# A decoder block with 32 experts: attention's order of work, the hgrn share in three products, and the first expert's rows per tile

## Time and profile before

| | us |
|---|---|
| median of 3 runs | 1307.71 (1305.7 to 1308.83) |
| the profiled execution's own time | 1308.46 |
| its span, first to last instruction | 1306.6 |
| PE busy in the span | 1248.9 (96%) |
| DVE, ACT, POOL busy | 538.1, 238.5, 135.8 |
| mean granted TensorE clock | 0.988 of 2.4 GHz |
| DMA, mean over the span | 345 GB/s |

### The profile page before, as it was taken

How to read it: one execution, slowest core, us unless ns; L and a number is a source line. 1 busy time by engine, 2 the same in 40 slices (tenths; PEclk the granted TensorE clock), 3 DMA queues, 4 the chain that set the end, 5 groups by cost and what they waited for, 6 DMA issues and landing times.

```text
span 1306.6 us, 33478 instructions
## 1 busy us (share of the span) xinstructions
PE 1248.9 (96%) x14751; PEld 726.3 (56%) x14752; DVE 538.1 (41%) x1045; ACT 238.5 (18%) x485; POOL 135.8 (10%) x144
## 2 busy tenths in 40 slices
PE   6999999999999999999999999999999999999994
PEld 5888876675357565555444455444445454545442
DVE  5767646566424524223242333333333333242424
ACT  6364424421011111010010100010000000010102
POOL 0000001100022221221010101001010101010002
PEclk9999999998999999999999999999999999999997
DMA  9523219027899999999999999999999999999993
GB/s 294 163 65 91 72 45 408 2 114 300 348 395 417 423 415 423 411 415 424 424 424 423 424 424 422 426 422 422 423 424 423 423 424 424 424 423 425 424 390 141
DMA packets 69402, 450.87 MB, mean 345 GB/s; under 512 B 6921, under 2 KB 36077, under 8 KB 44576
## 3 DMA queue, kind: packets, MB, share of 16 engines
q1 hardware_dynamic: 64832, 438.59, 81.5%
q0 software_dynamic: 4416, 10.02, 2.4%
HBM read 441.46 MB, written 9.31 MB: 345 GB/s over the span
## 4 chain that ended last, share of the span: by engine, by line
PE 62%; DMA 32%; DVE 2%; issue 1%; ACT 1%; SPq 0%; DVEq 0%
DMA w_raw_pair<-w_down 29%; PE psum L1945 24%; PE psum L1963 14%; PE psum L1698 8%; PE psum L1695 3%; DMA w_raw_pair<-w_up 3%; PE psum L1974 2%; PE psum L1784 2%; PE psum L1832 1%; PE psum L1808 1%; PE psum L1936 1%; PE psum L1771 1%; PE psum L1849 1%; DMA x_rows<-x 1%; PE psum L2018 1%
## 5 line engine op out<-in xcount | busy, mean ns | idle before, releaser
L1945 PE MATMUL psum<-w_raw_pair,x_slots_turned 128*32 128x512 f32 x4928 | 550.4, 593 | 1.0 <-DMA w_raw_pair<-w_up 0.8
L1945 PEld LDWEIGHTS psum<-w_raw_pair,x_slots_turned 128*32 128x32 f32 x4928 | 208.8, 110 | 280.4 <-issue 218.9
L1963 PE MATMUL psum<-w_raw_pair,a_slots 128*32 128x256 f32 x4992 | 288.3, 380 | 11.7 <-DMA w_raw_pair<-w_down 10.6
L1963 PEld LDWEIGHTS psum<-w_raw_pair,a_slots 128*32 128x32 f32 x4992 | 186.3, 110 | 103.5 <-DMA w_raw_pair<-w_down 15.3
L1522 DVE TENSOR_TENSOR x_rows<-x_rows,psum 128x1024 f32<-128x1024 f32 x106 | 124.6, 1218 | 269.5 <-PE psum L1974 269.5
L845 ACT ACTIVATE lin<-psum 128x768 f32<-128x768 f32 (+1 forms) x32 | 22.5, 704 | 579.3 <-PE psum L1945 579.3
L1491 DVE STREAM_TRANSPOSE a_slots<-glu 128x768 f32<-128x768 f32 (+1 forms) x31 | 26.3, 849 | 202.6 <-PE psum L1963 202.6
L1486 DVE STREAM_TRANSPOSE x_slots_turned<-gathered_quarters 128x256 f32<-128x256 f32 x74 | 43.2, 628 | 113.7 <-PE psum L1945 113.0
L640 POOL COPY gather_quarters<-row_quarters 128x2 int32 (+1 forms) x30 | 16.4, 547 | 691.6 <-DVE x_slots_turned L1486 659.4
L1974 PEld LDWEIGHTS psum<-y_part_group,token_sel 32*128 32x128 f32 x2016 | 63.5, 184 | 42.7 <-issue 42.7
L645 POOL DMA_INDIRECT gathered_quarters<-normed_rows,gather_quarters x74 | 75.0, 1014 | 39.2 <-POOL gather_quarters L640 25.8
(11 more groups left out here) (290 smaller groups left out, 1045.9 us busy)
## 6 DMA issues: line engine op xcount, KB each, us to landing
w_raw_pair<-w_up SPq DMA_DIRECT2D x128, 2048.0 KB, 37.7
w_raw_pair<-w_down SPq DMA_DIRECT2D x64, 2048.0 KB, 37.9
w_in_raw<-w_in SPq DMA_DIRECT2D x28, 512.0 KB, 3.7
w_buf<-w_out SPq DMA_DIRECT2D x4, 1024.0 KB, 8.5
expert_rows<-zero_rows SPq DMA_DIRECT2D x5, 512.0 KB, 6.9
x_rows<-x SPq DMA_DIRECT2D x4, 512.0 KB, 5.2
x_rows<-x SPq DMA_DIRECT2D x1, 2048.0 KB, 17.4
normed_rows<-h_rows SPq DMA_DIRECT2D x4, 512.0 KB, 2.6
```

What stands on the lines that cost most here:

```text
L1945: ins = pe.matmul(U[quarter(j), g, :], slots, up_columns(w, j), start=False, stop=(c == UPC - 1))
L1963: ins = pe.matmul(banks[quarter(j), g, :], slots[:, g, 2 * c + h, :], raw[q.slot(m)][:, at_w:at_w + 256], start=False, stop=(c == DNC - 1 ...
```

## The change

Three edits in one. (1) Scores go into three buffers instead of two; the scores of heads 0 and 1 are made behind av's first slice, in recurrence head 3, and so are their maxima and exponentials; later scores are made in halves of two row tiles, a head ahead; PE turns the probabilities of head h + 1 before the pv product of head h. DVE waits for x_again before its loop over the heads, where it stood before the first add. (2) `hgrn_share` is made in three float32r products instead of one float32 product: ACT makes high parts of G and of the recurrence's half of w_out (GH, WGH), POOL the low parts (GLo, WOL[:, 0]). The shares are taken in the order 0, 2, 4, 6, 1, 3 in heads 2 to 7, share 5 before oT and share 7 behind it. GH and WGH lie where two pairs of the first expert's weights go, so SP issues these two (`FIRST 2` and `FIRST 4`) only when share 7 is full, ahead of G2. (3) The slot matrices are made for tiles 0 and 1 before DVE's last x2 add, and for 2 and 3 after the last choice; the first expert's rows are gathered tile by tile between the logits; `order` moves behind the second up chunk, and on DVE `order_experts` behind the turning of the rows.

The diff, cut to its core:

```diff
@@ -210,7 +210,10 @@
         junk = over("x_sq", [P, D], g0)
         ZR = over("zero_rows", [P, D], hg0)
-        E = over("scores", [P, 2, 1280], fk0)
+        E = [over(f"scores{n}", [P, 1280], (fk0, fk0 + 5120, hg0 + 40960)[n]) for n in range(3)]
+        WGH = over("w_hgrn_high", [P, 2, HH, 512], hg0 + 16384, F32R)
...
+        def scored_in(h):
+            pair, tiles = ((h + 2) // 2, (2, 3)) if h % 2 == 0 else ((h + 3) // 2, (0, 1))
+            return ((2 * pair, 2 * pair + 1), tiles) if pair < AH // 2 else ((), ())
         def pair_scores(h):
-            return [("qk", g, i) for g in (h, h + 1) for i in range(TT)]
-        jobs += pair_scores(0)
-        SHARES = {h: h - 1 for h in range(1, AH)}
-        W_OUT_AFTER = (1, 2, 5, 6)
+            heads, tiles = scored_in(h)
+            return [("qk", a, i) for i in tiles for a in heads]
+        share_order = [n for half in range(2) for n in range(half, 2 * TT, 2)]
+        SHARES = dict(zip(range(2, AH), share_order))
+        BEFORE_OT, BEHIND_OT = share_order[AH - 2:]
+        W_HGRN_AFTER, W_OUT_AFTER = (0, 0, 1, 2), (3, 4, 5, 6)
+        jobs += pair_scores(-1) + [("pt", 0, c) for c in range(3)]
         for h in range(AH):
-            jobs += [("pt", h, c) for c in range(3)]
...
-            if h % 2 == 0 and h + 2 < AH:
-                jobs += pair_scores(h + 2)
+            jobs += pair_scores(h)
+            if h + 1 < AH:
+                jobs += [("pt", h + 1, c) for c in range(3)]
             jobs += [("pv", h)]
...
-        jobs += [("xa", n) for n in LATE_SHARES]
-        jobs += [("oT", j) for j in range(4)]
+        jobs += [("xa", BEFORE_OT)] + [("oT", j) for j in range(4)] + [("xa", BEHIND_OT)]
...
@@ -556,8 +574,10 @@
             load_pair(FIRST, 6, 6, 0)
             freed(sp, "gT", HH - 1)
             sp.dma_start(slot_rank[:, :], consts[:, CW:CW + P]).then_inc(S("slot_rank_in"), 16)
-            for n in range(0, 6, 2):
-                load_pair(FIRST, n, n, 0)
+            load_pair(FIRST, 0, 0, 0)
+            full(sp, "xa", BEHIND_OT)
+            load_pair(FIRST, 2, 2, 0)
+            load_pair(FIRST, 4, 4, 0)
...
             pool.memset(ZR[:, :], 0.0).then_inc(S("zero_rows"), 1)
+            for h in range(HH):
+                pool.wait_ge(S("g_high"), h + 1)
+                pool.tensor_tensor(GLo[:, h, :], G[:, h, :], GH[:, h, :].bitcast(F32), ALU.subtract).then_inc(S("g_low"), 1)
+            for m in range(4):
+                n, k = m // 2, m % 2 * 2
+                pool.wait_ge(S("w_hgrn_high"), m + 1)
+                pool.tensor_tensor(WOL[:, 0, n, k:k + 2, :], Wb[:, 0, n, k:k + 2, :], WGH[:, n, k:k + 2, :].bitcast(F32),
+                                   ALU.subtract).then_inc(S("w_hgrn_low"), 1)
...
                     hgrn_exps(act, h + 1)
+                if h == HH - 1:
+                    exps(0)
                 projected(h, 1)
+                if h == HH - 1:
+                    exps(1)
...
-                for c in range(3):
-                    if c == 1:
-                        continue
+            def probs_turned(h):
+                for c in (0, 2):
                     full(act, "pt", h, c)
                     if h >= 2:
                         full(act, "pv", h - 2)
                     lo, hi = (0, 512) if c == 0 else (1024, 1280)
                     act.activation(PTs[:, h % 2, lo:hi], bank("pt", h, c)[:, 0:hi - lo], ACT.Copy
                                    ).then_inc(free_sem("pt", h, c), 1)
-                if h in W_OUT_AFTER:
-                    m = W_OUT_AFTER.index(h)
+            probs_turned(0)
+            for h in range(HH):
+                freed(act, "gT", h)
+                act.activation(GH[:, h, :], G[:, h, :], ACT.Copy).then_inc(S("g_high"), 1)
+            for h in range(AH):
+                if h + 1 < AH:
+                    probs_turned(h + 1)
+                if h + 2 < AH:
+                    exps(h + 2)
+                for m in range(4):
                     n, k = m // 2, m % 2 * 2
-                    act.wait_ge(S(f"w_attn{n}"), 16)
-                    if m == 0:
-                        full(act, "o", HH - 1)
...
+            def masked_max(h, tiles):
+                for i in tiles:
+                    full(dve, "qk", h, i)
+                    n = TT * (h % 4) + i
+                    if h >= 3:
+                        full(dve, "pt", h - 3, 2)
+                    dve.tensor_tensor_reduce(E[h % 3][:, EOFF[i]:EOFF[i] + P * (i + 1)], bank("qk", h, i)[:, 0:P * (i + 1)],
+                                             cst("pairs")[:, (TT - 1 - i) * P:], 1.0, -3e38, ALU.add, ALU.max,
+                                             mx[:, n:n + 1]).then_inc(free_sem("qk", h, i), 1)
+                    freed(dve, "qk", h, i)
+                    dve.tensor_scalar(nmx[:, n:n + 1], mx[:, n:n + 1], -DH ** -0.5, None, ALU.mult
+                                      ).then_inc(S("neg_max"), 1)
             dve.wait_ge(S("c_rest"), 16)
             decays(0)
...
+                    masked_max(0, range(TT))
+                    masked_max(1, range(TT))
...
-                    masked_max(h + 2)
+            masked_max(2, (0, 1))
+            probs_turned(0)
+            masked_max(3, (0, 1))
+            dve.wait_ge(S("x_again"), 16)
+            for h in range(AH):
+                heads, tiles = scored_in(h)
                 if h in SHARES:
-                    if SHARES[h] == 0:
-                        dve.wait_ge(S("x_again"), 16)
                     add_share("xa", SHARES[h])
-                if h % 2 == 0 and h + 2 < AH:
-                    masked_max(h + 2)
+                if heads:
+                    masked_max(heads[0], tiles)
+                if h + 1 < AH:
+                    probs_turned(h + 1)
+                if heads:
+                    masked_max(heads[1], tiles)
...
                 dve.wait_ge(S("attn_high"), j + 1)
                 dve.scalar_tensor_tensor(OTL[:, j, :], bank("oT", j), agc[:, j:j + 1], OTH[:, j, :].bitcast(F32),
                                          ALU.mult, ALU.subtract).then_inc(free_sem("oT", j), 1)
+            add_share("xa", BEHIND_OT)
...
+            def slots_of(tiles):
+                cols = slice(tiles[0] * NE, (tiles[-1] + 1) * NE)
+                dve.wait_ge(S("selected"), tiles[-1] + 1)
+                link(dve.scalar_tensor_tensor(LG[:, 5, cols], bank("pos")[:, cols], 1.0, LG[:, 2, cols], ALU.add, ALU.mult))
+                for i in tiles:
+                    dve.tensor_scalar(SEL[:, i, :], slot_rank[:, :], LG[:, 5, i * NE:i * NE + 1], -1.0, ALU.subtract, ALU.is_equal
+                                      ).then_inc(sel_ready, 1)
...
+                if i == TT - 1:
+                    dve.wait_ge(S("slot_rank_in"), 16)
+                    dve.wait_ge(S("placed"), TT - 2)
+                    slots_of((0, 1))
                 add_share("x2", i, 1)
...
+            slots_of((TT - 2, TT - 1))
...
                 a_rows(p, n, As)
-            order_experts()
             slot_values()
...
                 ins = dve.transpose(xq[:, g, :, :], Xp[:, g, :].rearrange("p (i k) -> p k i", k=DK))
             ins.then_inc(t_free, 1)
+            order_experts()
+            next_rows()
             ordered()
-            next_rows()
             gates()
...
@@ -1703,6 +1768,14 @@
                 for j in range(4):
                     project(g, j)
+            def scores(heads, tiles):
+                for i in tiles:
+                    for g in heads:
...
+                    for j in range(4):
+                        freed(pe, "aq", j)
+                        freed(pe, "ak", j)
+                    scores((0, 1), range(TT))
...
             def hgrn_share(n):
-                if n == 0:
-                    for h in range(HH):
-                        freed(pe, "gT", h)
-                    pe.wait_ge(S("w_hgrn0"), 16)
-                    pe.wait_ge(S("w_hgrn1"), 16)
-                i = n // 2
+                i, half = n // 2, n % 2
+                pe.wait_ge(S("g_low"), HH)
+                pe.wait_ge(S("w_hgrn_low"), 2 * half + 2)
                 o = begin("xa", n)
-                for k in range(HH):
-                    ins = pe.matmul(o, G[:, k, i * P:(i + 1) * P], Wb[:, 0, n % 2, k, :], start=(k == 0), stop=(k == HH - 1))
+                for first, rows, w_rows in ((True, GH, WGH[:, half, :, :]), (False, GH, WOL[:, 0, half, :, :]),
+                                            (False, GLo, WGH[:, half, :, :])):
+                    for k in range(HH):
+                        ins = pe.matmul(o, rows[:, k, i * P:(i + 1) * P], w_rows[:, k, :], start=(first and k == 0),
+                                        stop=(rows is GLo and k == HH - 1))
                 ins.then_inc(full_sem("xa", n), 1)
-            attn_scores(0)
-            for h in range(AH):
+            def probs_turned(h):
                 pe.wait_ge(S("probs"), TT * (h + 1))
```

(38 more changed lines are left out.)

110 lines of the change are left out of this document (45 added, 65 removed).

## The result

The changed kernel takes 1323.5 us (median; 1321.1 to 1325.6), the kernel before 1306.7 on the same chip: the ratio is 1.0128, with a 95% interval of 1.0111 to 1.0146, so 14.5 to 19.1 us slower. A second set of runs of the same code gave 1.0131 (1.0113 to 1.0149). The forecast was 1314.7 and its range ended at 1320: the direction came, the size didn't. The profiled execution took 1322.9 and its span is 14.4 us longer than that of before.

The account below looks back on a forecast made before the run. The prediction took the chain of waits, chiefly PE's up to the first up product, as the bound, with the weight stream at its limit later. Terms +10.8 - 4.7 + 0.9 = +7.0 us gave 1314.7 us, range 1305 to 1320.

Parts of the forecast that it names:

- The first wait: Ahead of all attention heads: DVE waits for x, landing at 212.8 us, so PE stands 11.5 us, till 213.5.
- Rival (a): Transfers aren't held up by those ahead of them: x lands early, G2 takes some 5 us; 1296 us; 10%.
- Rival (d): The clock stays at 1.2 GHz behind waits through the heads' small products and first logits: 1320 us; 12%.
- The attention and G2, +10.8: Attention to first logits: oT 0.9 us later, G2 13.2 us behind two pairs; first logits 10.8 us late.
- the two long waits: PE's new waits, for x in attention and for G2 before the first x2 add: 11 and 5 us.
- The first expert's rows, -4.7: Router stage: half the last norm and row products moved earlier, so turning the rows starts sooner; 4.7 us gained.
- up to 1 us, within this term: DVE's wait for the last rows' store to normed_rows behind two pairs, ahead of turning: at most 1 us.
- order, +0.9: `order` moved behind the second up chunk now lies on PE's path: 0.9 us more.
- Rival (b): The weight stream hides the change, since DMA sets the end: 1308 us; 8%.
- What comes ahead of the first up product moves the end one for one: Until 366 us the weight stream follows PE, so changes before the first up product (318.3 us) shift the end equally.

Follow-up runs that it names:

- after: The changed kernel itself, as measured and profiled against the kernel before: 1323.5 us, ratio 1.0128.
- store_first: The changed kernel with pairs SECOND 2 and SECOND 4 issued behind the store of the last normed rows instead of ahead of it: ratio 1.0107.
- x_wait_late: The changed kernel with DVE's wait for x moved from ahead of head 0 to ahead of the first add of a share: ratio 1.0033.
- g2_first: The changed kernel with only the issue of G2 moved ahead of the pairs FIRST 2 and FIRST 4: ratio 1.0060.
- all_three: The changed kernel with the edits of store_first, x_wait_late and g2_first together: ratio 0.9926 to the kernel before.
- one_pair_one_product: one_pair_ahead with the shares as one float32 product again, without the copies and subtractions for high and low parts: ratio 0.9925.
- one_pair_ahead: all_three with SECOND 2 ahead of the last rows' store again and SECOND 4 still behind it: ratio 0.9911.
- after_again: The changed kernel run and traced once more with nothing changed: ratio 1.0131 to the kernel before.
- low_part_last: one_pair_ahead with a share's three products reordered, w_out's low part last, each waiting only for what it reads: ratio 0.9888, median 1293.6 us.
- low_last_x_early: low_part_last with x's second load issued behind the recurrence half of w_out, ahead of the attention half: ratio 0.9893.

## Why the prediction was wrong in size

What held. The first wait: x landed at 213.3 (forecast 212.8), DVE waited for it ahead of all heads, PE stood 12.3 us (11.5), and the first two low parts of w_out were ready at 221.6 (221.5). From share 0 to the end of pv 7 it was 40.1 us in the forecast and 40.1 in the trace (223.6 to 263.7): the new share is 2.8 us, and the three stalls between heads are gone. POOL's four subtractions took 4.95 us, 1.2 each, and ended at 202. G2 took 13.16 us behind its two pairs (13.2), and the first x2 add waited for it. Rival (a) fell with that, in three places: x, G2 and the store all landed as late as what was ahead of them in the queue makes them. Rival (d), the clock, was right in its mechanism and was the nearest to the time.

What failed, term by term, with the trace of after against the earlier trace rows:

- **The attention and G2, +10.8: it was +14.9** (logits of tile 0 at 296.3, 14.9 us later than before, 0.4 of it there at k_end_rows already). Share 0 came 2.0 us later than forecast (223.6 in the chain for 221.6), since behind PE's wait turns and pv 1 ran at half clock: 2.39 and 3.20 us where the later ones took 1.31 and 2.34. That gave oT 268.6 for 266.7, +2.8 instead of +0.9. Behind oT's own 2.1 us wait the clock fell again: oT's 2.44 us and share 7's 3.88 for the forecast 2.0 and 2.8, +1.5. And the two pairs take SP 0.9 us to issue before G2's own issue; the forecast had left that out. These are 1.9, 1.5 and 0.9: 4.3 us, as much as the whole error of the term (4.1). The forecast held 1 us for the clock, and said that each wait would be followed by a stretch at half; it priced only the two long waits and not the one at oT, and the products behind the wait for x too low. Behind G2 the clock was at half too (0.50 in 288 to 292), but there the first logits waited for ACT, and it cost nothing.
- **The first expert's rows, -4.7: they gave more, and the wait counted as within them cost more.** PE's row products ended at 326.2; 0.2 us later the transposes could have begun, as they did in store_first (326.51 and 326.68). So without the store they would stand at 326.4, 9.2 us behind the 317.16 of before, and the term is 9.2 - 14.9 = -5.7: the clock was at full speed for all four tiles' rows. But the prediction put the store's wait at "up to 1 us, within this term". It is a term of its own: 329.3 - 326.4 = 2.9 us.
- **What that wait left behind: nothing in the sum, 1.7 us in the trace.** The first up chunk ran at a clock of 0.65 and took 4.46 us for 24 products; 2.78 in store_first.
- **order, +0.9:** 0.8 us, between 338.53 and 339.31. Right.

The sum by the trace is 14.9 - 5.7 + 2.9 + 1.7 + 0.8 = 14.6, and the spans differ by 14.4.

The failed step of the prediction is thus how the waits were priced: the length of each was read well where it was asked for (x, G2), but the third transfer behind pairs was waved through, though it is the same case as G2 by the same row (slot_ranks), 0.5 MB behind 4.2 MB issued 9 us earlier, and cost 2.9 us; and three stretches of half clock (behind x, at oT and in the first up chunk), about 5 us in all, were given 1.

Rival (b), that the stream hides it, was wrong as priced: moves ahead of the first up product went through to the end in x_wait_late, g2_first and all_three. But it seems right in one case: store_first bought its 4.3 us with an empty queue and kept 2.7. The traces agree, with 1 to 2 us more from the first chunk to the end; by the times it is not shown. "What comes ahead of the first up product moves the end one for one" then holds only as long as the pairs are issued as early as before.

As to the parts of the change: with the waits mended, the rows are worth 4.8 us. For the products in three parts no gain is shown: 1.8 us within the noise, nothing ahead of oT and 0.7 us behind it by the traces. Yet GH and WGH are what puts the two pairs ahead of G2, and the low parts are what share 0 waits for. Attention's new order of work was undone in no run, but one_pair_one_product has it beside shares in float32 as before: counted from k_end_rows its oT starts at 92.0 us where the kernel before has 101.1, and of these 9.1 us 7.3 are left at the first logits. Most of the 11.6 us between one_pair_ahead and the kernel before is thus this part; which of its steps gives it (third buffer, early scores, turns ahead of pv, order of the shares) stays open.

## What to carry to other kernels

A transfer that something waits for took as long here as everything issued ahead of it in its queue: for each small load or store, add up the bytes ahead of it and their GB/s, and do it for all of them, not for the one that caught the eye. Three waits of 12, 13 and 3 us made a change lose 1.3% that gains 0.7% without them. Where a wait must stay, put ahead of it the work that doesn't need it (two of three products here), which took away the wait and the lowered clock behind it together. And a prefetch put behind a small transfer should keep as many bytes ahead as the small one can bear: one pair here delayed nothing, two did; that none costs time in the stream is likely, but not shown.

## What the runs showed of the hardware

**The clock behind a wait.** PE stood 12.2 to 12.4 us for x and then worked with short gaps, in four executions with the same code up to there. The granted clock was back at 2.4 GHz 6 to 8 us after PE had begun again in three of them (after, after_again, store_first: at 222, 221 and 221), and 15 us after in g2_first (230). The price was some 2 us in after and 3.5 more in g2_first. No run here controls it. Shorter waits were sometimes enough too. At oT PE waited 2.11 to 2.12 us in ten traces: in five the clock fell and oT took 2.44 to 3.61 us (after, after_again, store_first, low_part_last, low_last_x_early), in five it didn't and oT took 1.96 to 1.97. Behind the 2.3 us ahead of share 0 it fell in all four traces that have them. So a range of a forecast for this kernel has to hold some 5 us for the clock alone, and two single traces can differ by as much.

**DVE beside POOL.** A product of two tiles of 128x256 in SBUF takes DVE 0.42 us. Where it came while one of POOL's subtractions (2.4 us each) was at work it took 1.3 to 2.0 in every trace of a changed kernel, here in x_wait_late, with POOL's subtractions from 205.2 to 212.4:

```profile
208.19 1.94 DVE L1285 TENSOR_TENSOR attn_sq<-attn_rows 128x256 f32<-128x256 f32 x1
210.16 0.42 DVE L1286 TENSOR_REDUCE small<-attn_sq 128x4 f32<-128x256 f32 x1
...
221.18 0.42 DVE L1285 TENSOR_TENSOR attn_sq<-attn_rows 128x256 f32<-128x256 f32 x1
```

The reduction right behind it, with one input, is not slowed although POOL is still at work. (The Trainium skill, SBUF — State Buffer, section "SBUF: two separate sides": of a DVE operation with two SBUF inputs and a GpSimd operation that reads SBUF, whichever starts first has the shared port pair for its whole instruction, and the other waits. The rows agree in kind: 1.5 us of wait and 0.42 of work.) Here it cost nothing that the chains show, since DVE had slack; where POOL takes over work to relieve DVE it belongs in the sum.
